# A fused transformer kernel: table copies, clock keepers and modulation chunks in another order, and a renumbered gather ring

## What is computed

```python
mod_x = (silu(c) @ w_mod + b_mod)                     # six vectors: sh1, sc1, gt1, sh2, sc2, gt2
px = split(modulate(rms_norm(x, norm1), sh1, sc1) @ w_in)
na_x = neighbourhood_attention(px[0], px[1], px[2], k_ctx, v_ctx, na_rpb)
hg_x = hgrn2_mixer(px[3:], pc[3:], ...)               # a recurrence in both directions
x = x + gt1 * (concatenate([na_x, hg_x]) @ w_out)
x = x + gt2 * peer_ffn(modulate(rms_norm(x, norm2), sh2, sc2), ...)
# peer_ffn: keys pick 128 of 16384 experts for each token;
a = gelu(einsum('tpkd,td->tpk', u[idx], t))
out = einsum('tpk,tpkd->td', g * a, v[idx])
```

## Time and profile before

| | us |
|---|---|
| median of 3 runs | 3511.51 (3508.32 to 3514.45) |
| profiled execution | 3522.56 |
| its span | 3520.8 |
| PE busy | 3024.0 (86%) |
| DVE busy | 2070.3 (59%) |
| ACT busy | 834.3 (24%) |
| POOL busy | 703.5 (20%) |
| DMA, mean rate over the span | 241 GB/s |

### The profile page before, as it was taken

One profiled execution on the slowest core, in us unless ns is written; L12 is line 12 of the kernel. 1 busy time (PEld: TensorE's weight loads), 2 busy tenths in 40 slices (PEclk: granted clock), 3 DMA queues, 4 the chain that ended last, 5 costly groups with the idle time before them and its releaser, 6 DMA issues.

```text
span 3520.8 us, 35290 instructions
## 1 busy us (share of the span) xinstructions
PE 3024.0 (86%) x12520; PEld 2047.1 (58%) x12520; DVE 2070.3 (59%) x3646; ACT 834.3 (24%) x2176; POOL 703.5 (20%) x682
## 2 busy tenths in 40 slices
PE   7999888987777777777777789979999999899998
PEld 5886677762222222222222257667888777778876
DVE  3224785567776764684444455356875465668743
ACT  2112432222222222222222231142120102422201
POOL 0002452014444443343433311000000000100000
PEclk9999999999999999999999999989999999999999
DMA  6999896769999999999999942202333231023332
GB/s 220 317 290 296 242 293 218 234 252 421 421 421 421 408 418 422 413 414 419 419 417 421 415 197 90 78 1 80 99 96 90 78 114 54 12 80 95 95 90 72
DMA packets 154613, 847.89 MB, mean 241 GB/s; under 512 B 15392, under 2 KB 15648, under 8 KB 87648
## 3 DMA queue, kind: packets, MB, share of 16 engines
q0 software_dynamic: 79360, 563.38, 39.3%
q1 hardware_dynamic: 75104, 282.57, 25.9%
HBM read 841.70 MB, written 136.31 MB: 278 GB/s over the span
## 4 chain that ended last, share of the span: by engine, by line
PE 57%; DMA 27%; DVE 8%; issue 4%; ACT 3%; SPq 0%; ACTq 0%; POOL 0%; DVEq 0%; POOLq 0%
DMA RHI_f<-peer_uv,XC 19%; PE PS L204 13%; PE PS L206 13%; PE PS L205 13%; PE PS L822 7%; DMA AR<-peer_uv,XC 5%; DMA RING<-in_wstream 3%; PE PS L597 1%; PE PS L617 1%; DVE AR L1678 1%; DVE RING_r L1471 1%; DVE AR L1608 1%; ACT HC L1315 1%; PE PS L634 1%; DVE AR L1620 1%
## 5 line engine op out<-in xcount | busy, mean ns | idle before, releaser
L822 PE MATMUL PS<-AR,HC 128*128 128x512 f32 x1536 | 726.5, 618 | 256.9 <-ACT HC L1315 256.9
L204 PE MATMUL PS<-AR_r,RHI 128*128 128x512 f32 x1888 | 751.5, 398 | 26.6 <-DVE RING_r L1471 8.9
L206 PE MATMUL PS<-AR_r,RING_r 128*128 128x512 f32 x1888 | 737.7, 391 | 0.0
L822 PEld LDWEIGHTS PS<-AR,HC 128*128 128x128 f32 x1536 | 284.2, 194 | 698.5 <-ACT HC L1315 403.2
L1678 DVE SCALAR_TENSOR_TENSOR AR<-AR 128x1024 f32<-128x1024 f32 x384 | 470.1, 1225 | 366.8 <-DMA AR<-peer_uv,XC 366.2
L205 PE MATMUL PS<-AR_r,RHI 128*128 128x512 f32 x1504 | 586.2, 390 | 0.0
L488 POOL DMA_INDIRECT AR<-peer_uv,XC x384 | 400.3, 1042 | 729.1 <-PE PS L822 547.9
L1469 DVE CAST RHI<-RING 128x1024 fp32r<-128x1024 f32 x256 | 178.4, 697 | 485.4 <-DMA RING<-in_wstream 482.8
L204 PEld LDWEIGHTS PS<-AR_r,RHI 128*128 128x128 f32 x1888 | 356.2, 189 | 111.0 <-issue 21.2
L206 PEld LDWEIGHTS PS<-AR_r,RING_r 128*128 128x128 f32 x1888 | 355.8, 188 | 74.4
L1471 DVE TENSOR_TENSOR RING_r<-RING,RHI 128x1024 fp32r<-128x1024 f32 x256 | 315.8, 1234 | 8.8
(11 more groups left out here) (337 smaller groups left out, 3457.9 us busy)
## 6 DMA issues: line engine op xcount, KB each, us to landing
RING<-in_wstream SPq DMA_DIRECT2D x304, 512.0 KB, 3.6
peer_uv<-in_peer_u SPq DMA_DIRECT2D x56, 1024.0 KB, 14.7
peer_uv<-in_peer_v SPq DMA_DIRECT2D x56, 1024.0 KB, 16.6
peer_uv<-in_peer_v POOLq DMA_DIRECT2D x8, 1024.0 KB, 11.9
peer_uv<-in_peer_u POOLq DMA_DIRECT2D x8, 1024.0 KB, 11.9
AR<-peer_uv,XC POOLq DMA_INDIRECT x384, 13.5
XL<-in_xl SPq DMA_DIRECT2D x1, 2048.0 KB, 8.1
RHI_f<-peer_uv,XC POOLq DMA_INDIRECT x128, 13.5
```

The costliest lines, as they stand in the source:

```text
L204: pe.matmul(out, sh, mh, start=start, stop=False)
L206: return pe.matmul(out, sl, mh, start=False, stop=stop)
L822: mm = pe.matmul(bank(2 * (tt % 2) + x), DIAG[:, n % NDIAG, :], ROWS_UV[n % NROW][:, D + 512 * x:D + 512 * x + 512], start=(j == 0), stop= ...
```

## The change

Six edits. (1) `COPIES_AFTER`: eight of the 112 copies on SP's queue move. Chunks 26, 28, 32, 34, 38, 40, 44 and 46 of the projections are followed by one copy instead of two, and chunks 82, 85, 88, 91, 94, 97, 100 and 103 by two instead of one. (2) The 32 modulation chunks are placed anew: before the first direction none (was 6), behind its groups four; before the second four (was 6), behind its groups two; behind the head sums six (was four ahead of them). (3) 36 clock keepers stand before the first direction, 4 instead of 6 behind each direction's groups, and 4 instead of 8 ahead of the output projection. (4) The sum of head h-1 is made after the products of head h, the last one at the end; the two `turn_rows` move behind barrier 6. (5) VectorE splits each of the last four rows of `MIX` as soon as it is gated, ahead of the chunks of "out" and of the barrier. (6) The first four slots of the gather ring lie where the query projection's input was, the next two in the high parts of the chunk ring, the last two where the keys and the queries are, and only from gather 6 on is `pk_s` waited for.

```diff
--- before.py
+++ after.py
@@ -73,9 +73,9 @@
     if _c < FIRST["q"] + 3:
         _more = 0
     elif _c < FIRST["mod2"]:
-        _more = 2 if _c % 2 == 0 or _c % 3 == 0 else 1
+        _more = 2 if _c % 3 == 0 or _c in (20, 22) else 1
     else:
-        _more = 2 if _c % 4 == 0 and _c < FIRST["out"] else 1
+        _more = 2 if _c % 4 == 0 and _c < FIRST["out"] or _c % 3 == 1 and _c >= FIRST["out"] else 1
     COPIES_AFTER[_c] = range(_n, _n + _more)
     _n += _more
 assert _n + NA_HEADS // 2 * NCB == COPIES
@@ -305,8 +305,9 @@
         JUNK = [ar(28672 + 1024 * j, 1024) for j in range(2)]
         IDX = XCF[:, 0:512].bitcast(U32)
         GATE, RAW, GA = XCF[:, 512:1024], XCF[:, 1024:1536], XCF[:, 1536:2048]
-        ROWS_UV = [ar(4096 + 2 * D * j, 2 * D) for j in range(6)] + [
-            RHI_F[:, 2 * j:2 * j + 2, :].rearrange("p a b -> p (a b)") for j in range(2)]
+        ROWS_UV = [ar(8192 + 2 * D * j, 2 * D) for j in range(4)] + [
+            RHI_F[:, 2 * j:2 * j + 2, :].rearrange("p a b -> p (a b)") for j in range(2)] + [
+            ar(4096 + 2 * D * j, 2 * D) for j in range(2)]
         WEIGHT = HCF[:, 1152:1664]
         NDIAG = 8
         DIAG = HCF[:, 128:128 + NDIAG * P].rearrange("p (a b) -> p a b", a=NDIAG)
@@ -478,11 +479,12 @@
             pool.wait_ge(uv_copied, 16 * (COPIES - NA_STEPS))
             pool.wait_ge(uv_copied_late, 16 * NA_STEPS)
             pool.wait_ge(chunk_used, FIRST["wq"] + 16)
-            pool.wait_ge(pk_s, 16)
             for i, (tt, lo, hi) in enumerate(PARTS):
                 pool.wait_ge(pk_idx, i + 1)
                 for j in range(lo, hi):
                     n = SLOTS * tt + j
+                    if n == 6:
+                        pool.wait_ge(pk_s, 16)
                     if n >= NROW:
                         pool.wait_ge(row_used, n - NROW + 1)
                     pool.indirect_dma_start(ROWS_UV[n % NROW], None, PEER_UV,
@@ -730,7 +732,10 @@
 
             for d in range(2):
                 s = hg[d]
-                modulate(6)
+                if d == 0:
+                    keep_clock(5, 36)
+                else:
+                    modulate(4)
                 after(pe, s, "ready", 1, 1)
                 for x in range(16):
                     half = x % 2
@@ -744,7 +749,8 @@
                     mm.then_inc(s["a"], 1)
                     if x % 2 == 1:
                         modulate(1)
-                keep_clock(5, 6)
+                modulate(4 if d == 0 else 2)
+                keep_clock(5, 4)
                 for n, b in enumerate(HG_BLOCKS):
                     if n == 2:
                         after(pe, s, "p", 16, 16)
@@ -764,6 +770,11 @@
                     mm.then_inc(s["u"], 1)
                 barrier(pe, 4 + d)
 
+            def head_sum(h):
+                pe.wait_ge(ho["sq"], h + 1)
+                pe.matmul(bank((4, 5, 1, 0)[h]), ONES[:], HLF[:, 2048 + 512 * h:2560 + 512 * h], start=True,
+                          stop=True).then_inc(ho["sum"], 1)
+
             for h in range(HG_HEADS):
                 for n in range(TT):
                     u = (TT * h + n) * P
@@ -773,15 +784,14 @@
                         mm = pe.matmul(bank(h, P * n, P), SS[d][:, h, n, :], QE[d][:, u:u + P], start=False,
                                        stop=(d == 1))
                 mm.then_inc(ho["o"], 1)
-            modulate(4)
-            for h in range(HG_HEADS):
-                pe.wait_ge(ho["sq"], h + 1)
-                pe.matmul(bank((4, 5, 1, 0)[h]), ONES[:], HLF[:, 2048 + 512 * h:2560 + 512 * h], start=True,
-                          stop=True).then_inc(ho["sum"], 1)
+                if h >= 1:
+                    head_sum(h - 1)
+            head_sum(HG_HEADS - 1)
+            modulate(6)
+            barrier(pe, 6)
             turn_rows(1, 3)
             turn_rows(2, 4)
-            barrier(pe, 6)
-            keep_clock(1, 8)
+            keep_clock(1, 4)
 
             tiles(FIRST["out"], KT, MIXS, "mix1", main, n2, follow=rms(n2))
             passing(pe, 7)
@@ -1646,12 +1656,13 @@
                 dve.wait_ge(ho["root"], h + 1)
                 steps.done(dve.tensor_tensor(o, o, r, ALU.mult))
                 steps.wait()
-                dve.scalar_tensor_tensor(MIX[:, 4 + h, :], o, par("hg_norm")[:, h:h + 1], G[:, h, :], ALU.mult, ALU.mult)
+                steps.done(dve.scalar_tensor_tensor(MIX[:, 4 + h, :], o, par("hg_norm")[:, h:h + 1], G[:, h, :], ALU.mult,
+                                                    ALU.mult))
+                steps.wait()
+                split_mix(4 + h)
             first_chunks("out")
             barrier(dve, 6)
 
-
-            split_mix(*range(4, KT))
             for n in (1, 2):
                 steps.done(add_bias(n, n + 2))
             steps.wait()
```

## The result

| | before | changed |
|---|---|---|
| median, us | 3512.64 (4 runs, 3508.32 to 3514.45) | 3537.64 (4 runs, 3527.30 to 3542.33) |
| ratio | | 1.0070, interval 1.0046 to 1.0093 |
| profiled execution, us | 3522.56 | 3527.30 |
| span, us | 3520.8 | 3525.5 |
| PE, DVE, ACT, POOL busy, us | 3024, 2070, 834, 704 | 3026, 2071, 835, 702 |

The change costs 25 us; 27.0 was forecast over the median then known, 3511.51. The busy times are the same, so all of it is waiting. The two profiled executions differ by only 5 us because the one of before (3522.56) was slower than the four timed runs of its kernel, and that of the change was the fastest of its four.

The account below looks back on a forecast made before the run. The gathers' length is fixed by full DMA engines, so only their start moves, tied to SP's queue of chunks and copies. 1.4 + 13.8 + 6.0 + 9.1 - 3.3 = +27.0 us, 3538.5 on the median, range 3520 to 3554.

Parts of the forecast that it names:

- The copies' pace: SP's queue: 4.15 us a copy behind the recurrent stage (3.8 to 4.3), 5.5 for chunk with copy after idle time.
- First direction: First direction of the recurrence: keepers for six chunks ahead -7.1 us, four chunks ahead of the transposes +5.4.
- Second direction: Second direction: first masked copy's 5.32 us wait goes, chunk 73 late ahead of the transposes; +1.4 us at heads' start.
- The head stage: Head sums and modulation: six chunks start later, chunk 82 lands at +48.2, output product at +53.2 instead of +39.4; +13.8 us.
- Output chunks: Output projection: two more copies ahead of chunk 90 make it 5 us late, tile 86 waits 1 us; +6.0 us.
- Query chunks: Query stage: 11 chunks and 14 copies between chunks 92 and 103 take 71.3 us instead of 62.2; +9.1 us.
- The gather's wait, -3.3: First gather: no longer waits for the last key scores, starts about 1 us after the indices instead of 4.4; -3.3 us.
- fifth rival: Gathers' start: the moved wait is worth nothing, since the indices come last anyway; no separate chance, counted in the sum.
- the queue keeps up: SP's queue: copies at the gathers' pace, 2.5 us, nothing waits for chunks 73, 90 or 103; 3510 us, chance 0.06.
- chunks don't wait for copies: SP's queue: a chunk is served beside the copies, landing 3.7 us after issue; 3504 us, chance 0.06.
- the partial case: SP's queue: quicker when loaded evenly, 3.6 us a copy, stalls at 73 and 90 nearly vanish; 3523 us, chance 0.17.
- Worse: TensorE: each wait drops its clock, following tiles run at half speed, copies at 4.4 us; +42, 3553 us, chance 0.09.

Follow-up runs that it names:

- after_again: The changed kernel run once more without edit, for a second profile: 3542.27 us, ratio 1.0073.
- only_copies: The kernel before with only the new table of copies (the eight moved copies): 3521.93 us, ratio 1.0024.
- before_again: The kernel before run once more without edit, for a second profile: 3514.37 us.
- only_heads: The kernel before with sums between head products, four chunks behind them, turned rows behind the barrier, four keepers, MIX splits ahead of it: 3518.43 us, ratio 1.0003.
- only_directions: The kernel before with only the two directions' modulation chunks and keepers placed anew, leaving six chunks ahead of the head sums: 3532.10 us, ratio 1.0043.
- no_copies_78_81: The changed kernel with the four copies behind chunks 78 to 81 issued behind chunk 51 instead: 3527.91 us, ratio 1.0036.
- chunks_for_keepers: The changed kernel with four resident modulation chunks replacing the 36 keepers ahead of the first direction, none behind its groups: 3526.71 us, ratio 1.0034.

## Why the prediction was right, and where it was not

**Size and sign: right.** 3538.5 was forecast, 3537.64 measured. The reason holds too: a chunk lands behind the copies issued before it, and the copies' pace is the price. That the medians agree within 1 us is luck. From the first running sum to the first gather (A to E) the changed kernel is 16.0 us longer over the first pair of profiles and 27.2 over the second, where the sum has 27.0, and single executions of it took 3527.30 to 3546.04 us.

**The copies' pace: right.** In the changed kernel chunks 79 and 82 land at 589.5 and 605.3, 5.3 us for a chunk with its copy (5.7 in `after_again`), where the prediction had 5.5. In the full queue of the second direction chunks 63 and 77 land at 485.5 and 565.5; 14 chunks of 1.2 us and 18 copies lie between, 3.5 us a copy, below the 3.8 of the earlier trace rows.

**Eight copies leave the projections, 0: right.** The first running sum starts between 389.9 and 395.8 us in all profiles; `only_copies` has 391.0, the kernel before 393.5 twice.

**First direction: right.** The first masked copy comes 13.5 us after the running sums' start instead of 20.7 (-7.1 forecast); from there to the second direction's sums it takes 70.6 us instead of 66.3, and 63.9 in `before_again` (+5.4 forecast, +4.3 and +6.7 measured).

**Second direction: its sum nearly right, its place wrong.** Forecast was +1.4 us at the heads' start by a stall at chunk 73 ahead of the transposes. A is 0.5 us shorter than before in the first pair of profiles and 2.9 longer in the second. In the first profile chunk 73 landed at 543.7, not at 547.9, and nobody waited for it. In `after_again` the forecast wait is there, with 1.54 us:

```profile
548.90 1.94 PE L619 MATMUL PS<-RING,CS 128*32 128x128 f32 x16 [1.54 <-DMA RING<-in_wstream]
```

But in both the late start of the queue was felt first at the head of the direction: chunks 62, 63 and 65 came 2.83, 1.87 and 3.04 us late, and in `after_again` chunks 62 and 63 2.22 and 3.16. So the 5.32 us wait of the second direction's first masked copy didn't go but shrank to 1.65 (4.16 in `after_again`). From that copy to the heads it took 70.0 us for 64.0, and 68.1 for 63.9 in the second pair. By the prediction's prices 2.4 of this are the two chunks less two keepers; the waits for the ring in that stretch are 3.0 us for 1.3, and 1.5 for 0.9; the rest, 1 to 2 us, stays open. The step that failed is that the 5.32 us wait "goes" and that chunk 73 is the next thing late: it followed only the last chunk, and not the ones whose users come first.

**The head stage: size right, its cause partly misread.** Forecast +13.8; B grew by 12.0 to 15.0 over the pairs of profiles. Chunk 82 landed 45.9 us after the heads' start, forecast 48.2; the output product stood at +51.4, forecast +53.2. The prediction laid the later start of the chunks to the sums now ahead of them; `only_heads`, which has these sums ahead too, pays 1 to 3 us in B. `only_directions`, with six chunks ahead of the sums, pays 10 to 11. The cost is the two further chunks behind the heads, which make 80 to 82 the third to fifth chunk of a burst, and the copies in that burst (`no_copies_78_81`: B 39.9).

**Output chunks: size right, place wrong.** Forecast +6.0; C grew by 5.4 and 5.6, and by 4.7 in `only_copies`. Chunk 90 was to come 5 us late and tile 86 to wait 1 us. Measured it is the other way round: chunk 90 came 0.81 us late (1.63 in `after_again`, 1.91 in `only_copies`), while chunk 86 landed 35.8 us after the output product's start instead of 31.6, so that chunk 90, issued when 86 is used, was asked for 10.5 us after chunk 89 instead of 6.3.

**Query chunks: too large.** Forecast +9.1; D grew by 2.6 and 7.2, and by 7.8 in `only_copies`. The prediction let the queue set the pace from chunk 92 on. But the DMA share was 0.86, not full, and chunk 103 was issued 62.2 us after chunk 92 in both profiles of the change, as before. Only a backlog at the end is new: chunk 103 lands 6.4 and 9.3 us after its issue, 3.7 before. From the landing of 92 to that of 103 it took 65.0 and 67.7 us, forecast 71.3, before 62.2.

**The gather's wait, -3.3: size right (E 4.6 to 1.1), cause wrong.** In `only_copies` E is 1.1 without the edit: with the copies late, TensorE is done about when the indices are, or before. So the prediction's fifth rival, that the moved wait is worth nothing, nearly holds in the changed kernel, and 2.6 us or more of E's 3.5 belong to the copies' term: over D and E the change costs -0.9 and +3.7 us, forecast +5.8.

**The rivals.** That the queue keeps up and that chunks don't wait for copies are both excluded by the 19.9 us of chunk 82. One execution of the changed kernel in ten, 3527.30 us, came near the partial case's 3523. "Worse" named the clock after each wait: it is there after three of the waits (3.41, 3.52, 3.31 us where 1.93 is usual, at a granted clock of 0.54 to 0.57), but for one chunk each time, and not after the 1.87 us wait (1.94 us at 1.00).

What stays open: whether the 36 keepers bought anything; no run leaves them out alone. `chunks_for_keepers` also takes four chunks out of the first direction's tail, so its gain is that of both together. Nor is it shown what makes two executions of one kernel differ by up to 11 us ahead of the gathers.

## What to carry to other kernels

Where a ring of weights and bulk copies share a queue, list each chunk's issue and landing. Resident chunks belong into TensorE's waits: using them is what asks for the next ones, and with filler work there instead the queue stays empty until the first chunk is used (407.67 us here). Do not put a burst of new chunks, each with a copy behind it, in front of a barrier; keep the copies behind those chunks out, but find a stretch with room for them first, and compare its idle time (14 us here) with what the copies need.

## What the runs showed of the hardware

The DMA engines are fully busy at very different rates: 1.00 to 1.01 at 418 GB/s in the gathers, and 0.99 at 328 GB/s with chunks and copies from HBM to HBM. At the gathers' rate the 1 MB of a copy would take 2.5 us, and 5.0 if its reading and its writing were counted each. Counting a chunk at the prediction's 1.2 us, a copy took 3.5 us in the second direction's full queue and 4.1 and 4.5 behind the heads (chunks 79 to 82 of the two profiles of the change), which neither gives. What sets it was not tried.
